# Differential attention with Q left unscaled and the bias scaled by Q's root, a new order around the first head, and a split first load of pooling weights

## What is computed

```
q = (rmsnorm(x) @ w_q) -> (seq, head, 2, 64);  q = rmsnorm_64(q, q_norm) * 64**-0.5
k = (rmsnorm(x, kv_norm) @ w_k) -> (seq, head, 2, 64);  k = rmsnorm_64(k, k_norm)
sc = q_c . k_c + rel_bias[bucket(i - j), head], masked to j <= i      for c in 0, 1
a  = softmax(sc_0) - lam * softmax(sc_1);   o = a @ v;   o = rmsnorm_128(o) * (1 - lambda_init)
```

## Time and profile before

| | before |
|---|---|
| median of 3 runs | 958.41 us (958.12 to 958.52) |
| profiled execution, its own time | 958.15 us |
| its span, first to last instruction | 956.4 us |
| TensorE (PE) busy | 944.9 us |
| VectorE (DVE) busy | 683.5 us |
| ScalarE (ACT) busy | 460.1 us |
| GpSimd (POOL) busy | 84.0 us |
| mean granted TensorE clock | 1.000 |

### The profile page before, as it was taken

One profiled execution on the slowest core, in us unless ns is written; L12 is line 12 of the kernel. 1 busy time (PEld: TensorE's weight loads), 2 busy tenths in 40 slices (PEclk: granted clock), 3 DMA queues, 4 the chain that ended last, 5 costly groups with the idle time before them and its releaser, 6 DMA issues.

```text
span 956.4 us, 13002 instructions
## 1 busy us (share of the span) xinstructions
PE 944.9 (99%) x5135; PEld 809.9 (85%) x5135; DVE 683.5 (71%) x979; ACT 460.1 (48%) x587; POOL 84.0 (9%) x68
## 2 busy tenths in 40 slices
PE   8999999999999999999999999999999999999998
PEld 6878998998899898788888888888888888888887
DVE  5876766666676687977777787667766676677685
ACT  7634334334333437586666775435433433433441
POOL 3101000100000000122222220000000000000000
DMA  7427682385457444143223223324776269238534
GB/s 254 128 87 222 141 254 89 88 233 164 116 111 215 149 72 132 45 116 87 74 86 88 82 77 107 104 89 100 209 215 180 93 126 264 90 89 224 172 88 132
DMA packets 99442, 128.94 MB, mean 135 GB/s; under 512 B 3304, under 2 KB 61976, under 8 KB 99392
## 3 DMA queue, kind: packets, MB, share of 16 engines
q1 hardware_dynamic: 85216, 98.31, 31.4%
q0 software_dynamic: 14080, 29.91, 16.9%
q10 hardware_dynamic: 96, 0.02, 0.0%
HBM read 126.11 MB, written 4.74 MB: 137 GB/s over the span
## 4 chain that ended last, share of the span: by engine, by line
PE 90%; DVE 4%; ACT 3%; issue 1%; DMA 1%; SPq 0%; DVEq 0%; ACTq 0%
PE bank L1515 28%; PE bank L1517 28%; PE bank L1516 28%; PE bank L1761 2%; PE bank L1771 2%; DMA raw<-in_pool_w_dram 1%; PE bank L1797 1%; DVE w_low L970 1%; DVE work L1396 0%; ACT work L799 0%; ACT w_high L613 0%; ACT a_high_buf L634 0%; PE bank L1686 0%; DVE a_low_buf L979 0%; PE bank L1651 0%
## 5 line engine op out<-in xcount | busy, mean ns | idle before, releaser
L1515 PE MATMUL bank<-h_high_buf,w_high 128*128 128x512 f32 x640 | 252.5, 394 | 1.4 <-DVE w_low L970 1.4
L1517 PE MATMUL bank<-h_high_buf,w_low 128*128 128x512 f32 x640 | 249.4, 390 | 0.0
L1516 PE MATMUL bank<-h_low_buf,w_high 128*128 128x512 f32 x640 | 249.2, 389 | 0.0
L1515 PE MATMUL bank<-a_high_buf,w_high 128*128 128x256 f32 (+1 forms) x592 | 184.1, 311 | 2.1 <-DVE a_low_buf L1237 1.4
L1517 PE MATMUL bank<-a_high_buf,w_low 128*128 128x256 f32 (+1 forms) x592 | 183.0, 309 | 0.0
L1516 PE MATMUL bank<-a_low_buf,w_high 128*128 128x256 f32 (+1 forms) x592 | 182.9, 309 | 0.0
L970 DVE TENSOR_TENSOR w_low<-raw,w_high 128x2048 fp32r<-128x2048 f32 (+1 forms) x58 | 125.4, 2162 | 53.4 <-ACT w_high L676 33.6
L1515 PEld LDWEIGHTS bank<-h_high_buf,w_high 128*128 128x128 f32 x640 | 120.2, 188 | 29.1 <-DVE w_low L970 2.2
L1517 PEld LDWEIGHTS bank<-h_high_buf,w_low 128*128 128x128 f32 x640 | 120.1, 188 | 25.4
L1516 PEld LDWEIGHTS bank<-h_low_buf,w_high 128*128 128x128 f32 x640 | 120.3, 188 | 23.7
L685 ACT ACTIVATE work<-work 128x512 f32<-128x512 f32 x64 | 40.0, 632 | 175.9 <-DVE work L1037 175.9
...
## 6 DMA issues: line engine op xcount, KB each, us to landing
...
```

Of the source, the lines that this page charges most:

```text
L1515: pe.matmul(acc, w_hi, m_hi, start=start, stop=False, skip_group_check=onto)
L1516: pe.matmul(acc, w_hi, m_lo, start=False, stop=False, skip_group_check=onto)
L1517: return pe.matmul(acc, w_lo, m_hi, start=False, stop=stop, skip_group_check=onto)
```

## The change

Q is no longer multiplied by its inverse root. The inverse root of Q belongs to a query, and queries are the partitions of the scores, so it becomes a scalar per partition: ACT and DVE multiply the bias tile by Q's root beforehand (`bias_scale`, into `p1(i)` and `p2(i)`), DVE adds the unscaled scores to that and multiplies by `neg_rstd_q`, the negative inverse root. The copy of Q, the spread of its inverse root, its transposition back and `q_norm` are gone; `q_high` and `q_low` read the PSUM bank directly. The bias tile is loaded once both scalings of the head before have read it.

The first two heads are reordered: `turn_ksq(1)` stands between the first score pairs, `half_low_of` puts two half subtractions on DVE, the squares of x are added in four steps (1024, 1024, 1024, 512) between other work, `first_v_low` covers the first half of V's weights, and the pieces of `project` follow each other in another order. `norm_turn` of both MLPs moves from place (1, 4) to (1, 2). The first pooling group's weights have a DMA, an ACT copy and a subtraction of their own (a quarter of the unit instead of a half). The parameter transposition moves behind seven of the last tile's eight. In the last head, `o_low(0)` and `o_low(1)` come after `combine(last, 0)` and no longer in the body before. The masked value becomes -1e30.

```diff
-            sp.dma_start(raw[0][:, :].rearrange("p (g k n) -> p g k n", g=G, k=GD // P), pool_v).then_inc(w_landed[0], 16)
+            pool_raw = raw[0][:, :].rearrange("p (g k n) -> p g k n", g=G, k=GD // P)
+            sp.dma_start(pool_raw[:, 0:1], pool_v[:, 0:1]).then_inc(pool_first_landed, 16)
+            sp.dma_start(pool_raw[:, 1:], pool_v[:, 1:]).then_inc(w_landed[0], 16)
...
-                if h:
+                if h >= 2:
                     pool.wait_ge(half_high, h + 1)
...
-                    pool.wait_ge(s_taken, 8 * h)
+                    pool.wait_ge(bias_first, 4 * h)
+                    pool.wait_ge(bias_second, 4 * h)
                 pool.wait_ge(bias_spread, 16 * (h + 1))
...
-            act.wait_ge(w_landed[0], 16)
-            act.activation(w_high_buf[0][:, 0:UNIT // 2], raw[0][:, 0:UNIT // 2], ACT.Copy).then_inc(pool_half_high, 1)
+            act.wait_ge(pool_first_landed, 16)
+            act.activation(w_high_buf[0][:, 0:S], raw[0][:, 0:S], ACT.Copy).then_inc(pool_first_high, 1)
             mix_high(0)
             mix_high(1)
             copy_xt(0)
-            act.activation(w_high_buf[0][:, UNIT // 2:], raw[0][:, UNIT // 2:], ACT.Copy).then_inc(w_high, 1)
+            act.wait_ge(w_landed[0], 16)
+            act.activation(w_high_buf[0][:, S:], raw[0][:, S:], ACT.Copy).then_inc(w_high, 1)
...
-            def copy_q(n):
+            def q_high(n):
                 act.wait_ge(w_used, U_HEAD + 1 + 2 * n)
-                act.activation(qf, I[1][:, :], ACT.Copy).then_inc(qf_ready, 1)
+                act.activation(q_hi, I[1][:, :], ACT.Copy, scale=qk_gain[:, 0:1]).then_inc(q_high_done, 1)
...
+            def bias_scale(n, tiles):
+                act.wait_ge(t_landed, 16 * n + 16)
+                act.wait_ge(kq_rooted, n + 1)
+                for i in tiles:
+                    act.activation(p1(i), bias_of(i), ACT.Copy, scale=kq_root_buf[:, 8 + 2 * i:9 + 2 * i]).then_inc(bias_first, 1)
...
+            act.wait_ge(norm_turned, NORM_KV + 1)
+            bias_scale(0, range(TT))
             def head(h, first, last=False):
                 n = h + 1
+                if first:
+                    square_k(n)
+                    act.wait_ge(k_low_done, 1)
+                    copy_k(n)
...
-                square_k(n)
-                if first:
-                    act.wait_ge(kq_low, 1)
-                copy_k(n)
                 if not first:
+                    square_k(n)
+                    copy_k(n)
                     split_v(n)
-                split_high_first(n + 1, kq_landed(n + 1))
+                    split_high_first(n + 1, kq_landed(n + 1))
+                else:
+                    split_high_first(n + 1, kq_landed(n + 1))
                 if last:
                     o_high(0)
                     o_high(1)
                 square_q(n)
-                copy_q(n)
+                q_high(n)
                 at_highs(h, range(1))
                 kq_roots(n)
                 if not first:
                     o_roots(h - 1)
                 at_highs(h, range(1, 3))
+                bias_scale(n, (0, 1))
                 bring_table(ACT.Exp)
                 k_high(n)
-                q_high(n)
+                bias_scale(n, (2, 3))
...
+                    dve.wait_ge(w_high, U_HEAD + 2)
+                    dve.tensor_tensor(w_low_buf[0][:, 512:1024], raw[0][:, 512:1024], f32(w_high_buf[0][:, 512:1024]), ALU.subtract)\
+                       .then_inc(first_v_low, 1)
                 if l == 1 and q == NQ - 1:
                     take_last()
                 else:
                     take_4(l, q, 1)
                 if l == 0 and q == NQ - 1:
-                    split_low(U_HEAD + 1, 0, 1024)
+                    split_low(U_HEAD + 1, 0, 512)
...
-            dve.wait_ge(pool_half_high, 1)
-            dve.tensor_tensor(w_low_buf[0][:, 0:UNIT // 2], raw[0][:, 0:UNIT // 2], f32(w_high_buf[0][:, 0:UNIT // 2]), ALU.subtract)\
-               .then_inc(pool_half_low, 1)
+            dve.wait_ge(pool_first_high, 1)
+            dve.tensor_tensor(w_low_buf[0][:, 0:S], raw[0][:, 0:S], f32(w_high_buf[0][:, 0:S]), ALU.subtract)\
+               .then_inc(pool_first_low, 1)
...
-            def kq_sums(n, b):
-                kq_reduce(n, b[0], ksq_turned, 0)
-                kq_reduce(n, b[1], qsq_turned, 1)
+                sums = kq_sum_buf[:, :].rearrange("p (f g) -> p f g", f=2)
+                dve.tensor_tensor(sums, sums, kq_eps[:, :].unsqueeze(1).to_broadcast([P, 2, 8]), ALU.add).then_inc(kq_total, 1)
+            def kq_sums(n, k_bank, q_bank, first):
+                kq_reduce(n, k_bank, ksq_turned, 0)
+                if first:
+                    half_low_of(n + 1)
+                q_low(n)
+                kq_reduce(n, q_bank, qsq_turned, 1)
                 kq_add_eps(n)
+            def half_low_of(n):
+                dve.wait_ge(half_high, n)
+                dve.tensor_tensor(w_low_buf[1][:, 0:UNIT // 2], raw[1][:, 0:UNIT // 2], f32(w_high_buf[1][:, 0:UNIT // 2]), ALU.subtract)\
+                   .then_inc(half_low, 1)
...
-                for half, (dst, s) in enumerate(((ksq, k_spread), (qsq, q_spread))):
-                    dve.tensor_copy(dst.rearrange("p (g d) -> p g d", d=HD),
-                                    kq_rstd_buf[:, 8 * half:8 * half + 8].unsqueeze(2).to_broadcast([P, 8, HD])).then_inc(s, 1)
+                dve.tensor_copy(ksq.rearrange("p (g d) -> p g d", d=HD), kq_rstd_buf[:, 0:8].unsqueeze(2).to_broadcast([P, 8, HD]))\
+                   .then_inc(k_spread, 1)
+                dve.tensor_scalar(neg_rstd_q[:, :], kq_rstd_buf[:, 8:16], -1.0, None, ALU.mult).then_inc(neg_ready, 1)
+            def bias_scale(n, tiles):
+                dve.wait_ge(t_landed, 16 * n + 16)
+                for i in tiles:
+                    dve.tensor_scalar(p2(i), bias_of(i), kq_root_buf[:, 9 + 2 * i:10 + 2 * i], None, ALU.mult).then_inc(bias_second, 1)
...
-            def q_norm(n, b):
-                dve.wait_ge(q_turned, n + 1)
-                dve.tensor_tensor(qf, qf, b[:, :], ALU.mult).then_inc(qn_ready, 1)
...
+                dve.wait_ge(q_high_done, n + 1)
+                dve.scalar_tensor_tensor(q_lo, I[1][:, :], qk_gain[:, 0:1], f32(q_hi), ALU.mult, ALU.subtract).then_inc(q_low_done, 1)
...
+                dve.wait_ge(neg_ready, h + 1)
+                dve.wait_ge(bias_first, 4 * h + i + 1)
+                dve.wait_ge(bias_second, 4 * h + i + 1)
                 dve.wait_ge(s_done, 8 * h + 2 * i + 2)
                 dve.memset(wait_cell[0:1, i:i + 1], 0.0)
                 for c in range(2):
                     j = 2 * i + c
-                    t = p1(i) if c == 0 else p2_ring[i % 2][:, 0:P * (i + 1)]
-                    dve.tensor_tensor_reduce(out=t, in0=O[j % 4][:, 0:P * (i + 1)], in1=bias_tile[:, P * (3 - i):S],
-                                             scale=-1.0, scalar=-MASKED, op0=ALU.add, op1=ALU.min,
+                    t = p1(i) if c == 0 else p2(i)
+                    dve.tensor_tensor_reduce(out=t, in0=O[j % 4][:, 0:P * (i + 1)], in1=t,
+                                             scale=neg_rstd_q[:, j:j + 1], scalar=LARGEST, op0=ALU.add, op1=ALU.min,
...
-            prep_x(H_Q, a_high_buf, a_low_buf, C_MIX + KC)
-            for step, half in enumerate((4, 2, 1)):
-                dve.wait_ge(kv_squared, KC)
-                if step:
-                    dve.wait_ge(kv_summed, step)
-                dve.tensor_tensor(kv_sq[:, 0:half, :], kv_sq[:, 0:half, :], kv_sq[:, half:2 * half, :], ALU.add).then_inc(kv_summed, 1)
-            dve.wait_ge(half_high, 1)
-            dve.tensor_tensor(w_low_buf[1][:, 0:UNIT // 2], raw[1][:, 0:UNIT // 2], f32(w_high_buf[1][:, 0:UNIT // 2]), ALU.subtract)\
-               .then_inc(half_low, 1)
+            def kv_add(to, of, n):
+                dve.tensor_tensor(kv_sq[:, to:to + n, :], kv_sq[:, to:to + n, :], kv_sq[:, of:of + n, :], ALU.add).then_inc(kv_summed, 1)
+            dve.wait_ge(kv_squared, 4)
+            kv_add(0, 2, 2)
+            prep_x(H_Q, a_high_buf, a_low_buf, C_MIX + KC, range(4))
+            dve.wait_ge(kv_squared, KC)
+            kv_add(4, 6, 2)
+            prep_x(H_Q, a_high_buf, a_low_buf, C_MIX + KC, range(4, KC))
+            dve.wait_ge(kv_summed, 2)
+            kv_add(0, 4, 2)
+            dve.wait_ge(kv_summed, 3)
+            kv_add(0, 1, 1)
+            half_low_of(1)
...
+            q_low(0)
             norm_keep(NORM_KV, I[3])
             k_norm(0, O[0])
-            q_norm(0, O[1])
+            bias_scale(0, (0, 1))
+            k_low(0)
             take_v(0)
-            k_low(0)
-            q_low(0)
-            dve.wait_ge(w_high, U_HEAD + 4)
-            dve.tensor_tensor(w_low_buf[0][:, 0:1024], raw[0][:, 0:1024], f32(w_high_buf[0][:, 0:1024]), ALU.subtract).then_inc(second_v_low, 1)
+            bias_scale(0, (2, 3))
...
+                if first:
+                    split_low(U_HEAD + 3, 0, 1024)
...
```

(51 more changed lines are left out.)

91 lines of the change are left out of this document (44 added, 47 removed).

## The result

The kernel after takes 951.88 us in the median of 6 runs (951.55 to 953.34), the kernel before 958.38 beside it (958.12 to 959.07): 6.5 us less, ratio 0.9934, 95% interval 0.9924 to 0.9945. The forecast was 952.6, a gain of 5.8.

A forecast was written before the change was run, and what follows sets the result against it. TensorE, busy 944.9 of 956.4 us, was taken as the bound. Terms: -3.5 - 1.45 - 0.6 - 3.05 + 1.6 + 1.2 = -5.8, from 958.15 to 952.35, median 952.6 us; range 950.7 to 955.4.

The forecast's parts named there:

- Less work on TensorE: All eight heads: 32 transpositions of Q's inverse root go, 0.108 us each, 3.5 us less (upper end 4.2).
- Start: Up to the first pooling product: a quarter of the pooling weights is ready earlier, 1.45 us less, range 1.0 to 1.7.
- First MLP: `norm_turn` two products earlier removes the wait of 0.63 at 67.54: 0.6 us less; second MLP nothing.
- K, V and head 0: Where K, V and the first head begin: four waits of TensorE go (0.75, 0.5, 1.3, 0.5), 3.05 us less.
- New waits, head 0: First head: three new waits of TensorE, together 1.6 us more, ends 0 and 3.
- (a): Head 0: `turn_ksq(1)` between the first score pairs waits 0.6 us for ACT's square and copy of K.
- (b): Head 0: half subtraction and `q_low` ahead of Q's sums on DVE; K's spread about 0.5 us late for TensorE.
- (c): Head 0: ACT's two longer scalings delay the square of O; `turn_osq(0)` waits 0.5 us.
- The loop: Loop over the heads: DVE's and ACT's changed work costs TensorE nothing; a head takes 24.7 us, not 25.1.
- Last head: `o_low` made later: TensorE waits 0.8 for `o_low(0)`, then 0.4 and 0.2; put at 1.2 us more (0 to 1.8).
- POOL is first at the last scaling: Loop: DVE stands behind POOL, score pair 2 waits about 1.05 us a head, +6.3, 958.9; chance 0.10.
- POOL is first at both: Loop: both long DVE scalings wait for POOL, 1.5 us a head in seven heads, +10.5, 963.1; chance 0.04.

The follow-up runs named there:

- e9: Kernel after plus four superfluous transpositions a head (of V, into a free bank) right behind the scores, in seven heads: 954.18 us.
- e6: Kernel after with the first pooling group's weights in one transfer with the rest, copied and subtracted by halves again: 953.35 us.
- e7: Kernel after with the parameters' transposition and their copy back at their old places: 952.29 us.
- e5: Kernel after with `norm_turn` back at place (1, 4) in both MLPs: 953.91 us.
- e4: Kernel after with ACT's second half of the weights put between its two long scalings of the bias: 956.47 us.
- e8: Kernel after with `o_low(0)` and `o_low(1)` back in the last body, ahead of K's and Q's sums: 951.43 us.
- e2: Kernel after with four superfluous transpositions a head put back, behind the turn of K's reciprocals: 959.17 us.
- e3: Kernel after with ACT's second half of the weights put ahead of both long scalings of the bias: 955.91 us.
- e10: Kernel after with `o_low(0)` moved into DVE's gap ahead of the last head's scores: 952.8 us.

## Why the prediction was right

**Less work on TensorE: right, in size too.** Five heads of the loop, where TensorE has no gap in either kernel, are 0.47 us shorter each; the forecast had 0.43, e9's added four cost 0.33 to 0.39. The term of 3.5 stands between eight times 0.47 (3.8) and what e9 gives by its total time, 28 transpositions for 2.3 (0.08 each, 2.6 for 32).

**Start: right.** -1.63 for -1.45, inside its range. e6 takes all of it back at the first pooling product, so it needs the quarter; 0.4 of it needs the order around the parameters as well (e7). The forecast had that order at up to 0.25 for the square, and 0 to 0.3 for the transposition.

**First MLP: right in mechanism, too small.** The wait of 0.63 at 67.54 went, and e5 brings it back. From start to start that wait cost 0.79 (three matmuls up to it took 1.47 us instead of 0.68), and the matmul behind it 0.11 more. The stretch gained 1.01. The rest stands at the first output product: the matmuls around 101.03 in the kernel before are 0.20 and 0.22 apart instead of 0.12, under the size that the profile lists as a wait, and in the kernel after they are not. e5 has a step of 0.22 there again. What holds them is not shown. The second MLP was forecast at nothing. Against the kernel before that is what came out, but e5 shows that it needed its share of the edit: from the last head's scores to the end it takes 389.24 us for 388.20, so 1.0 of e5's 2.0 us lies there and 1.0 in the first MLP, as much as that stretch had gained.

**K, V and head 0: right, too small by 0.6.** All waits named went. (The fourth, on Q's low part, 0.48 at 418.85, stood in the next stretch of the table and went too.) No run puts this order back, so the term rests on the two profiles alone. The listed idle times of the first three, 0.75, 0.49 and 1.30, sum to 2.54. Added up from start to start, against the 0.23 us that a matmul of 512 columns takes in the middle of a product, TensorE lost about 4 us in that stretch before and 1 after. A wait costs more than its listed idle: the matmul ahead of it is drawn to its modelled end, 0.16 us past the point where the next could have started, and the one behind it takes 0.1 more.

**New waits, head 0: all three came, 1.62 us for 1.6.** (a) at L1783 behind ACT's copy of K, forecast 0.6, 0.50; (b) at L1802 behind K's spread, 0.5, 0.51; (c) at L1802 behind ACT's square of O, 0.5, 0.61. (The working of (a) gives 2.8 less 2.1, which is 0.7 and not 0.6.) The same understatement makes them cost more: the stretch to head 2 lost 0.67 where 0.23 was forecast. The two errors have opposite signs, and that they partly cancel is luck.

**The loop: right, and close.** No wait, a head at 24.64 for the forecast 24.7. DVE was first at the last scaling by 0.22 us, for 0.15 to 0.2. POOL's subtraction takes 2.49 instead of 2.38 to 2.40, not the 2.7 that was named as the mark; that length shows only where DVE is 0.03 ahead (e4, 2.69).

**Last head: right.** Three waits were forecast, 0.8, 0.4 and 0.2, which add up to 1.4, though the sum took 1.2. There are 0.50 for `o_low(0)` and 0.32 for `o_low(2)`, and a third that the profile doesn't list as idle, since it is hidden in the modelled end of the transpositions ahead of it. In the kernel after, a product starts at 578.42, 1.28 us behind the start of the ten transpositions ahead of it, instead of 1.01 (583.90 and 584.91 before). DVE's `o_low(4)`, the first of this pair, ends only shortly before; that it is what the product waits for is read from these times:

```profile
577.14 1.25 PE L1841 MATMUL bank<-ident,work 128*128 128x128 f32 x10
578.42 0.47 PE L1558 MATMUL bank<-a_high_buf,w_high 128*128 128x512 f32 x1
...
577.53 1.41 DVE L1004 SCALAR_TENSOR_TENSOR a_low_buf<-work,sub_gain,a_high_buf 128x512 fp32r<-128x512 f32 x2
```

The stretch lost 1.38. e8 takes 1.27 of that away, but pays for it in the body before, so that 0.45 is left.

**The rivals.** "POOL is first at the last scaling" is real and stands 0.22 us away: e2 meets it. Its price was 1.05 us a head; in e2 it is about 0.8 (a head is 1.23 longer, less the 0.39 that e9's four transpositions cost). "POOL is first at both" was forecast as the worse case at 1.5 us a head. e4 and e3 are that case. e4, with POOL 0.07 us ahead, costs 0.76 a head, of which 0.48 lie ahead of score pair 2, 0.19 ahead of pair 3 and 0.10 ahead of the next product. e3, with POOL 0.57 ahead, costs 0.26. The mechanism was right: the second scaling behind POOL adds 0.3 us, for 0.45 forecast. What was wrong is the size: the earlier POOL starts, the earlier it is through, and the price left that out. No run showed a slower side from there.

The Trainium skill, "SBUF — State Buffer", section "Who interferes with whom", says that whoever issues first keeps the other waiting for its whole instruction. With POOL first the trace agrees: a scaling lasts up to 2.60 us instead of 0.48 and ends 0.2 to 0.3 us behind POOL. With DVE first POOL is longer too, but by less than the two overlap: by 0.10 us where DVE's scaling runs on for 0.26 us, by 0.30 where it runs on for 0.45 (e4's first body). The same section says that a DVE instruction with two SBUF inputs contends with a GpSimd instruction that reads SBUF; e10 agrees, 2.87 us for 0.74, as L1408 did in the earlier trace rows. e10's expectation had that only as its rival.

Of the eleven variants none is clearly better than the kernel after. e8 lies 0.45 us under it, and its interval (0.9917 to 0.9944) overlaps.
